# Attention probabilities scaled on GpSimd between the splits of weights, scores kept negated, and group sums ordered by form

## What is computed

```python
def sink_probs(scores, sink):
    m = jnp.maximum(jnp.max(scores, axis=-1, keepdims=True), sink)
    p = jnp.exp(scores - m)
    return p / (jnp.sum(p, axis=-1, keepdims=True) + jnp.exp(sink - m))
# s = q . k / 8 + alibi bias, masked; o = sink_probs(s, sink) . v
```

```python
y = rmsnorm(y.reshape(b, l, SSM_GROUPS, SSM_INNER // SSM_GROUPS), norm_w.reshape(...))
```

## Time and profile before

| | us |
|---|---|
| median of three runs | 1904.31 |
| lowest and highest of them | 1900.27, 1904.8 |
| profiled execution | 1899.76 |
| its span, first to last instruction | 1898.0 |
| TensorE busy in it | 1799.6 |
| VectorE busy in it | 853.1 |
| GpSimd busy in it | 793.1 |

### The profile page before, as it was taken

One profiled execution on the slowest core, in us unless ns is written; L12 is line 12 of the kernel. 1 busy time (PEld: TensorE's weight loads), 2 busy tenths in 40 slices (PEclk: granted clock), 3 DMA queues, 4 the chain that ended last, 5 costly groups with the idle time before them and its releaser, 6 DMA issues.

```text
span 1898.0 us, 31359 instructions
## 1 busy us (share of the span) xinstructions
PE 1799.6 (95%) x13177; PEld 1705.3 (90%) x13177; DVE 853.1 (45%) x1649; ACT 640.7 (34%) x1148; POOL 793.1 (42%) x478
## 2 busy tenths in 40 slices
PE   6998998999999999998999999998999999999996
PEld 6997876998999999998888888787799899999996
DVE  6337887316312121138867676764613611212124
ACT  6326665325222121225323342332623412222221
POOL 1331210333646363541465665755133645545451
PEclk9999999999999999999899999999999999999998
DMA  6521110221222222221212111112022222222221
GB/s 230 181 67 57 62 62 30 67 90 65 81 79 84 83 79 89 78 88 61 67 38 66 59 54 60 45 65 99 23 84 73 72 85 78 90 78 87 80 79 72
DMA packets 42076, 146.57 MB, mean 77 GB/s; under 512 B 4816, under 2 KB 6480, under 8 KB 41680
## 3 DMA queue, kind: packets, MB, share of 16 engines
q1 hardware_dynamic: 40144, 140.59, 21.8%
q10 hardware_dynamic: 1792, 3.97, 0.6%
HBM read 138.13 MB, written 6.41 MB: 76 GB/s over the span
## 4 chain that ended last, share of the span: by engine, by line
PE 79%; DVE 13%; issue 3%; ACT 3%; POOL 1%; DMA 1%; SPq 0%; DVEq 0%; ACTq 0%; POOLq 0%
PE ps L917 66%; DVE u L1784 3%; PE ps L1287 1%; DVE mix L1427 1%; PE ps L900 1%; DVE x L1430 1%; PE ps L1052 1%; PE ps L1070 1%; DVE xp L1418 1%; PE ps L1156 1%; DVE prob L1554 1%; PE ps L1133 1%; DVE big_lo L1371 1%; DMA raw<-in_slabs 1%; PE ps L1081 1%
## 5 line engine op out<-in xcount | busy, mean ns | idle before, releaser
L1941 POOL TENSOR_TENSOR w_lo<-raw,w_hi 128x1024 fp32r<-128x1024 f32 x225 | 555.7, 2472 | 751.1 <-ACT w_hi L471 658.9
L917 PE MATMUL ps<-big_hi,w_hi 128*128 128x288 f32 x3552 | 786.4, 302 | 11.0 <-POOL w_lo L1941 3.1
L917 PE MATMUL ps<-big_hi,w_lo 128*128 128x288 f32 x3552 | 767.0, 297 | 0.0
L917 PE MATMUL ps<-big_lo,w_hi 128*128 128x288 f32 x3552 | 759.7, 297 | 7.5 <-DVE big_lo L1371 7.5
L917 PEld LDWEIGHTS ps<-big_hi,w_hi 128*128 128x128 f32 x3552 | 574.7, 189 | 22.5 <-issue 16.3
L917 PEld LDWEIGHTS ps<-big_lo,w_hi 128*128 128x128 f32 x3552 | 571.9, 189 | 12.8 <-DVE big_lo L1371 11.9
L917 PEld LDWEIGHTS ps<-big_hi,w_lo 128*128 128x128 f32 x3552 | 576.0, 189 | 0.1
L471 ACT ACTIVATE w_hi<-raw 128x1024 fp32r<-128x1024 f32 x242 | 255.2, 1056 | 480.1 <-DMA raw<-in_slabs 479.9
L1683 DVE TENSOR_TENSOR mix<-ps,mix 128x576 f32<-128x576 f32 x62 | 46.9, 757 | 306.3 <-PE ps L917 306.3
L1671 DVE SCALAR_TENSOR_TENSOR relu<-ps,rstd 128x576 f32<-128x576 f32 x60 | 45.4, 756 | 280.2 <-PE ps L917 280.2
L1984 POOL TENSOR_TENSOR hid<-relu 128x576 f32<-128x576 f32 x64 | 98.7, 1544 | 158.7 <-DVE relu L1671 158.5
(11 more groups left out here) (200 smaller groups left out, 1744.8 us busy)
## 6 DMA issues: line engine op xcount, KB each, us to landing
raw<-in_slabs SPq DMA_DIRECT2D x242, 512.0 KB, 3.4
bias<-in_alibi SPq DMA_DIRECT2D x12, 256.0 KB, 2.7
x<-in_x SPq DMA_DIRECT2D x2, 1152.0 KB, 8.3
out_h<-state ACTq DMA_DIRECT2D x4, 384.0 KB, 2.6
out_y<-x SPq DMA_DIRECT2D x2, 576.0 KB, 2.8
kms<-in_mk SPq DMA_DIRECT2D x2, 512.0 KB, 5.1
vms<-in_mv SPq DMA_DIRECT2D x2, 512.0 KB, 6.1
out_y<-x SPq DMA_DIRECT2D x1, 864.0 KB, 3.5
```

Source lines behind the costliest of these rows:

```text
L917: ins = pe.matmul(ps[:, bank + h, 0:hi_c - lo_c], w[:, s % RING, kt], a[:, k0 + kt, lo_c:hi_c], start=start, stop=stop, skip_group_check=True)
L1941: pool.tensor_tensor(w_lo[:, s % RING], raw[:, s % RING], w_hi[:, s % RING].bitcast(F32), ALU.subtract).then_inc(lo_done, 1)
```

## The change

Four things are changed.

1. In N, VectorE only adds and takes the reciprocal, and signals `inverted`; the multiplications of the probabilities are done by GpSimd, at its place N in the list, and signal `normed` from there.
2. GpSimd's splits in this stage are no longer one row of 12: one is done at every eighth K of the list, so each stands between multiplications.
3. In B the scale 1.0 becomes -1.0 and the maximum a minimum with negated sinks, so the stored scores and their extreme are both negated; the exponential gets `scale=-1.0` and the extreme as its bias. The sign change and `max_done` of this stage fall away, and E waits for `biased`. A small operation before the stage makes the negated sinks.
4. In the group sums the four products of 128 rows come first, then the four of 64 rows, with the two row halves in turn.

```diff
-                act.wait_ge(max_done, n_ + 1)
+                act.wait_ge(biased, n_ + 1)
...
-                    act.activation(ap, ap, ACT.Exp, bias=stat[:, r, 1, b:b + 1], accum_out=stat[:, r, 2, b:b + 1])
+                    act.activation(ap, ap, ACT.Exp, bias=stat[:, r, 0, b:b + 1], scale=-1.0, accum_out=stat[:, r, 2, b:b + 1])
...
+                        alone(pe)
                         for m in range(2):
                             for h in range(2):
-                                c0, c1 = h * HALF, (h + 1) * HALF
-                                o = ps[:, 4 + 2 * m + h, 0:HALF]
-                                r0 = m * HD
-                                alone(pe)
-                                pe.matmul(o, mats[:, 1], gsq[:, 2 * m, c0:c1], start=True, stop=False)
-                                ins = pe.matmul(o, mats[r0:r0 + HD, 1], gsq[r0:r0 + HD, 1, c0:c1], start=False, stop=True)
+                                pe.matmul(ps[:, 4 + 2 * m + h, 0:HALF], mats[:, 1], gsq[:, 2 * m, h * HALF:(h + 1) * HALF],
+                                          start=True, stop=False)
+                        for h in range(2):
+                            for m in range(2):
+                                half = slice(m * HD, (m + 1) * HD)
+                                ins = pe.matmul(ps[:, 4 + 2 * m + h, 0:HALF], mats[half, 1], gsq[half, 1, h * HALF:(h + 1) * HALF],
+                                                start=False, stop=True)
                         ins.then_inc(gsum_done, 1)
...
+            dve.tensor_scalar(minus_sink[:], par[:, C_SINK:C_SINK + 2 * TILES], -1.0, None, ALU.mult)
...
-                                                   bias[half, j, e, c0 + d:c1 + d], 1.0,
-                                                   par[half, sink:sink + 1], ALU.add, ALU.max,
+                                                   bias[half, j, e, c0 + d:c1 + d], -1.0,
+                                                   minus_sink[half, sink:sink + 1], ALU.add, ALU.min,
                                                    stat[half, r, 0, k:k + 1])
                 ins.then_inc(biased, 1)
-                sums = 2 if u else 1
-                dve.wait_ge(biased, n_ + 1)
-                dve.tensor_scalar(stat[:, r, 1, 0:sums], stat[:, r, 0, 0:sums], -1.0, None, ALU.mult).then_inc(max_done, 1)
...
+                if sink:
+                    dve.reciprocal(total, total).then_inc(inverted, 1)
+                    return
...
-            slabs_lo(TILES)
+            for kind, t in STEPS:
+                if kind == "K" and t % KT == KT - 1:
+                    slabs_lo(1)
+                elif kind == "N":
+                    r, u = t % 4, t % UNITS_J
+                    parts = [(0, P if u < 3 else 0, 2 * P), (1, 0, 2 * P)] if u else [(0, 0, P + DEC)]
+                    pool.wait_ge(inverted, t + 1)
+                    for b, c0, c1 in parts:
+                        ap = prob[:, r, b, c0:c1]
+                        ins = pool.tensor_scalar(ap, ap, stat[:, r, 2, b:b + 1], None, ALU.mult)
+                    ins.then_inc(normed, 1)
```

More of the change, by code:

```diff
@@ L255, in build @@
         eps = main.take("eps", [P, 1])
+        minus_sink = main.take("minus_sink", [P, 2 * TILES])
         main.p = (main.p + 31) // 32 * 32
@@ L362, in build @@
         max_done, exp_done, normed = sem("max_done"), sem("exp_done"), sem("normed")
+        inverted = sem("inverted")
         t_done, pt_done = sem("t_done"), sem("pt_done")
@@ L613, in exps @@
                         half = slice(e * DEC, (e + 1) * DEC)
-                        ins = act.activation(stat[half, r, 3, 0:1], stat[half, r, 0, 0:1], ACT.Exp, scale=-1.0,
+                        ins = act.activation(stat[half, r, 3, 0:1], stat[half, r, 0, 0:1], ACT.Exp,
                                              bias=par[half, C_SINK + 2 * q + e:C_SINK + 2 * q + e + 1])
                 else:
-                    ins = act.activation(stat[:, r, 3, :], stat[:, r, 0, :], ACT.Exp, scale=-1.0, bias=par[:, sink:sink + 1])
+                    ins = act.activation(stat[:, r, 3, :], stat[:, r, 0, :], ACT.Exp, bias=par[:, sink:sink + 1])
                 ins.then_inc(exp_done, 1)
@@ L651, in exps @@
                     n_, u = n.n + c, c % 3
-                    act.wait_ge(max_done, n_ + 1)
+                    act.wait_ge(max_done, n_ + 1 - UNITS)
                     rows = P if u else DEC
@@ L1552, in bias_max @@
                         half, e, k, c0, c1, d = slice(0, P), (u - 1) % 2, b, P if u < 3 and b == 0 else 0, 2 * P, 0
-                    sink = C_SINK + 2 * q + e
+                    sink = 2 * q + e
                     ins = dve.tensor_tensor_reduce(prob[half, r, k, c0:c1], ps[half, bank, k * 2 * P + c0:k * 2 * P + c1],
-                                                   bias[half, j, e, c0 + d:c1 + d], 1.0,
-                                                   par[half, sink:sink + 1], ALU.add, ALU.max,
+                                                   bias[half, j, e, c0 + d:c1 + d], -1.0,
+                                                   minus_sink[half, sink:sink + 1], ALU.add, ALU.min,
                                                    stat[half, r, 0, k:k + 1])
                 ins.then_inc(biased, 1)
-                sums = 2 if u else 1
-                dve.wait_ge(biased, n_ + 1)
-                dve.tensor_scalar(stat[:, r, 1, 0:sums], stat[:, r, 0, 0:sums], -1.0, None, ALU.mult).then_inc(max_done, 1)
             def normalise(n_, rows, parts, sink=True, sums=2):
@@ L1580, in norm @@
                 if u == 0:
-                    normalise(n.n + t, P, [(0, 0, P + DEC)], sums=1)
+                    normalise(n.n + t, P, [], sums=1)
                 else:
-                    normalise(n.n + t, P, [(0, P if u < 3 else 0, 2 * P), (1, 0, 2 * P)])
+                    normalise(n.n + t, P, [])
             def take_out(w):
```

## The result

The changed kernel takes 1925.87 us at the median of four runs (1923.74 to 1926.37), the kernel before 1903.26 in the same comparison: a ratio of 1.0118, 95% interval 1.0102 to 1.0134. It is **22.6 us slower**, above the range that was given.

What follows compares the result with a forecast made beforehand. TensorE, busy 1799.6 of 1898.0 us, was taken to bound the kernel. Attention +5.5 us and group sums -8.6 gave -3.1, so 1901.2 us against the median of 1904.31; range 1891 to 1913.

Steps and rivals of the forecast that it cites:

- the price of a multiplication on GpSimd: Attention stage: a moved multiplication takes 0.45 us for 256 columns and 0.35 for 128 on GpSimd.
- the ceiling: Upper bound on a GpSimd multiplication, from two-input products and a split: 0.62 us for 256 columns; attention then +12.6 us.
- The mechanism at u4: Attention, seven tiles: a split between u3 and u4 holds u4's add; transposes 1.2 us later, once 1.85, sum 9.0.
- 2.2 us before u2: Attention: what u2 costs if GpSimd takes 0.62 us for 256 columns.
- The slower rival: Attention: multiplications near or above 0.62 us bound every tile; whole +4.0 at 0.62, +11.6 (1915.9) at 0.80; chance 0.22.
- u3 in the first two tiles: Attention: the split between u2 and u3 ends before u3's add, since VectorE first takes out a query tile; nothing lost.
- The last two splits: Attention, after the ninth slab: splits between u4 and next u0 start sooner, removing waits before u0's transposes; 3.5 us gained.
- Held adds: Attention: a small VectorE add stands still until a running GpSimd split ends; if not held, the sum is 3 us lower.
- Removed sign changes: Attention: 60 sign changes, 21.4 us, leave VectorE; none of it counts by itself, u2's multiplication ends 0.1 us sooner.
- Group sums: Layer two, four times: ordering by form takes 3.28 us instead of 5.42; 8.6 us gained, 4.8 if half products do not overlap.

Runs made afterwards that it cites:

- neg_g_unshifted: Kernel before with scores kept negated and group sums ordered by form, multiplications on VectorE, the new tile placed so no other tile moves; 1888.95 us, ratio 0.9928.
- g_only: Kernel before with the group sums ordered by form, nothing else; 1894.42 us, ratio 0.9963.
- bcast: Changed kernel with the GpSimd multiplication written as a product of two tensors, the second the broadcast reciprocal; 1890.49 us, ratio 0.9944 to the kernel before.
- filler: Changed kernel with two dummy TensorE products of 512 columns ahead of each of nine long waits; 1918.21 us, ratio 1.0084 to the kernel before.

## Why the prediction was wrong

- **The step that failed is the price of a multiplication on GpSimd**: for 256 columns 0.45 us taken, 0.62 held for the ceiling, 0.923 measured. The ceiling came from a product of two tensors, and the broadcast form shows that line to be right: 0.613. The scaling by a column of factors is a costlier form than the product, though it reads one row instead of two. To take the two-input product as a ceiling for a one-input scaling was the error. (The Trainium skill, GPSIMD Engine Reference, Elementwise — side-by-side cycle accounting, gives 1.03 cycles of 1.2 GHz an element for small bodies. The trace does not agree for this scaling: 923 less 603 ns over 128 columns is 2.5 ns each, three such cycles.)
- **The mechanism at u4 was right.** Seven waits were named; seven came. In the step's own working four multiplications count, u3's two ahead of the split and u4's two behind it. With 0.923 for 0.45 it gives 1.2 + 4 x 0.47 = 3.1 each and 3.7 at the sixth slab, together 22.3. Measured before u4 are 2.05 to 2.26 and 3.03, together 15.8. The rest stands before earlier units of the same seven tiles, which the step does not count (the prediction has them apart, as 2.2 us before u2 at its ceiling): 1.06 before u2 in four of them, 0.41 and 0.2 before u1 and u3 in the other three, 6.1 in all. The tiles as wholes lose 21.9.
- **The slower rival held in kind**: it said 42 us per us that a multiplication takes. At 0.923 that is 5.5 + 0.473 x 42 = +25.4 in attention, where the waits grew by 21.7, and 1921.1 for the whole, where 1925.87 was measured. It had a chance of 0.22 and ended at 1915.9, since 0.80 was as far as it looked.
- **The clock was missing altogether**: up to 13.4 us by the stretches, 7.7 regained by filling the waits. No term of the sum asked what TensorE does behind a long wait. None of rows 1 to 10 shows such a wait, but the trace of before has one, in layer two, with the clock at its lower level behind it (order of time, then the stretches view):

```profile
921.14 0.62 PE L1246 MATMUL ps<-hs,mats 64*128 64x24 f32 x2 [4.59 <-DVE hs L1831]
...
920.00:924.00 4.00, 2.86 (x10) 0.50 0.01 2
```

- **u3 in the first two tiles: "nothing" was wrong, mostly by the price.** Two waits of 2.38 us stand there, where the kernel before had two of 1.1. The first of each, before and now:

```profile
146.04 0.66 PE L1070 MATMUL ps<-mats,prob 128*128 128x128 f32 x4 [1.12 <-DVE prob L1575]
...
148.09 0.33 PE L1072 MATMUL ps<-mats,prob 128*128 128x128 f32 x1 [2.38 <-POOL prob L2029]
```

  The split was over by then, as forecast, but u3's add comes behind the query tile that VectorE takes out of PSUM, its reciprocal at 145.95, and then the two multiplications take from 146.21 to 148.06. At the price taken, 0.90 for the pair, the wait would have been 1.4 us, 0.3 more than before; at the price measured it is 1.3 more in each of the two tiles. The waits stay at 2.38 with the splits behind u4 or on VectorE and fall to 1.72 with the broadcast product, so they are the multiplications' own.
- **The last two splits: right.** The waits before u0 fell from 4.0 to 0.9 us.
- **Held adds: right.** The add of 128 x 2 takes 446 ns at the mean of 48 and 2.38 when a split has just begun; the trace agrees with the rule of the Trainium skill (SBUF — State Buffer, SBUF: two separate sides), an exclusive lock held for the whole instruction.
- **Removed sign changes: undersized.** Costed at zero beside 0.1 of gain; with the multiplications on VectorE they are worth 5.5 us (`neg_g_unshifted` against `g_only`), of which 3.9 in the stage, but only 0.7 are left of that once the multiplications are on GpSimd.
- **Group sums: right**, 3.28 a time, 3.20 once; 7.5 us arrive of 8.6.

## What to carry to other kernels

An operation moved to an engine that is idle 85% of the time costs what one *unit* of it delays the next engine, not what it frees; bound its price by a row of the same form, and when there is none, measure the form before the schedule is built on it, and try its neighbours: here a broadcast product took two thirds of a scaling. Count what a long wait costs TensorE afterwards as well as during it, and look for a wait of that length elsewhere in the trace of before: here one stood in layer two. And when a part of a change gains more than its work, look at a stretch that it does not touch: here the stretch's own pace had changed with the addresses.

## What the runs showed of the hardware

- GpSimd, float32, in place, 128 partitions: scaling by a per-partition factor 603, 763 and 923 ns for 128, 192 and 256 columns; the same as a product with the broadcast factor 400, 506 and 613 ns.
- TensorE's granted clock fell to the 1.2 GHz level behind seven of nine waits of 2.05 to 3.03 us in the changed kernel's attention, and rose to 2.4 GHz again some microseconds later; behind the other two (2.05 and 2.26) it stayed. Elsewhere it fell behind one of 1.77 (`neg_g_unshifted`) and stayed behind one of 1.98 (`bcast`). With products in the long waits, so that none of over 1.2 us was left (`filler`), it stayed at 1.00. So the length of a wait alone does not decide, and what else does is not shown.
- The same dense stream of products of 288 columns runs at 133 or 129 ns each with the clock at 1.00, one pace for a whole stretch. At the addresses of the kernel before no execution shows the faster one; with the tiles shifted by 96 bytes in SBUF some do and some do not. Which tile matters, and what makes one execution take it and the next not, was not tried and stays open.
- Products of 64 rows in alternating halves, all of one form: eight records of 288 columns in 1.24 us, against 2.18 for 128 rows.
